# A token-mixing projection that applies the norm's token factor to its results instead of its input, on one core

## The chip, the cores and the metric

The kernel runs on one core of a Trainium2 chip, in float32. The metric is the device time of one execution in microseconds (us), as the median of several runs.

## What is computed

The reference is one layer of a decoder trunk on 256 tokens of width 2048. It has three sub-layers: a token mixer, a cross-attention into 256 memory tokens, and a gated MLP. The change touches the mixer, whose input is normed and then projected:

```
def rms_norm(x, g):
    y = xf * lax.rsqrt(jnp.mean(xf * xf, axis=-1, keepdims=True) + EPS)
    return (y * g)
z = rms_norm(x, ln_mix_pre) @ w_in      # columns: short conv, RWKV-7, retention, sparse attention, gates
```

The four groups of columns feed four mixers: a gated short convolution ("sc"), RWKV-7 ("rw", "zw", "za"; its recurrence is worked in chunks of 64 tokens, and its output is head-normed, scaled, given a bonus term and multiplied by a gate), retention ("rq", "rk", "rv", "rg") and sparse attention ("kv", "q"). The last group holds the merge gates ("g0" and the gates made in the merge loop), which go through a sigmoid. The norm has two factors: one for each input channel (g) and one for each token, rstd = rsqrt(mean(x²) + eps). The token factor is the same for all channels, so it may stand on the result: (x·rstd·g) @ w = rstd · ((x·g) @ w).

## The kernel before

Activations lie transposed, with channels on the 128 partitions and 256 tokens in the free dimension; x is 16 such tiles (`xT`). Every float32 product is made of three fast ones: a weight half is rounded by ScalarE ("high", L1179), VectorE subtracts that from the raw weight ("low", L1897), and TensorE multiplies high x (high and low of the input, side by side in 512 columns; L437) and low x high (256 columns; L442). ScalarE copies the second 256 columns of the bank out of PSUM (`mix_cross`, L1213), and VectorE adds them to the first (`evict`, L1952, which counts `chunk_out`).

A chunk is one tile of 128 output columns: 1 MB of weights, in two halves of 512 KB that cover 8 input tiles each. SyncE issues the loads (L336) in the order of the chunks, each half once the low part of the half two chunks earlier is done. The list `MIX` sets the order of the 78 chunks: 0 to 11 rw, 12 zw, 13 za, 14 and 15 rw, 16 to 27 sc, 28 to 33 kv, 34 to 37 cmp (a small product on the keys), 38 to 41 q, 42 to 45 rq, 46 to 49 rk, 50 to 57 rv (tokens on partitions, L407 and L410), 58 to 65 rg, 66 to 77 g0. On each engine `go(n, h)` stands in a list written out by hand and means "all halves before half h of chunk n"; what stands between two such calls is the mixers' own work. TensorE runs a chunk's matmuls once the chunk two before it is evicted.

The start (functions `gained`, `added`, `normed`, `x_low`, L1972 to 2025) goes: four quarters of x arrive; ScalarE squares them (L1170); VectorE multiplies two quarters by g (L1975) and sums the squares (L1981, L2004, L2006); TensorE sums over the partitions (L773); ScalarE takes the root (`std`, L1162), VectorE the reciprocal (L1884); VectorE norms x (L1988, L1888), ScalarE rounds it (L1191), VectorE makes the low part (L1996). Then TensorE can begin chunks 0 and 1, which are interleaved by quarters of the input (L450, L456).

The RWKV work is spread over chunks 4 to 45: the token shift (POOL `difference` L1762, DVE `token_shift` L1907), the key norm (ACT L1239, POOL L1767, PE `rw_kk`), the low-rank maps (`rw_lora`), the bonus sum (`rw_bonus`, L530, in the middle of chunk 20, which waits for L2094), the recurrence, and the ending of its output on VectorE: L2335 (times the reciprocal deviations), L2337 (four instructions, lnx_g and lnx_b), L2340 (plus bonus), L2343 (times the gate). Right after it VectorE works the attention units u = 0 to 7 in chunks 46 to 58: TensorE makes scores (L706, L707), VectorE the mask and the maximum (`unit_max`, L2252 to 2256), ScalarE the exponentials (L1360, L1363), VectorE scales them (`unit_scale`, to L2268), TensorE transposes them (`unit_T`, L714 to 716). The short convolution (L1784 to 1790) and one product of the retention's rotation (L1809, on 2048 columns) run on POOL. After the mixing chunks come the merge of three tiles and the merge loop over 13 tiles (four gate chunks and two branch chunks each, L894 and L903), the output projection, the cross-attention and the MLP, which the change leaves alone.

## Time and profile before

| | us |
|---|---|
| median of 3 runs | 2244.86 (2240.94 to 2255.99) |
| the profiled execution | 2244.42 |
| its span, first to last instruction | 2242.6 |
| TensorE busy with matmuls | 2190.3 |
| VectorE busy | 1503.8 |
| ScalarE busy | 1114.9 |
| GpSimd busy | 217.7 |

The profile is of one execution. Its busy time counts an engine's instructions, waits left out; its span is shorter than the execution's time by 1.8 us, which lie around it. A busy TensorE is not TensorE at its peak.

### The profile page before, as it was taken

Reading aid. Unit: us, or ns where it says so; the run is one execution under the profiler, and the core shown is the slowest. Engines: PE = TensorE matmul, PEld = TensorE weight load, DVE = VectorE, ACT = ScalarE, POOL = GpSimd, SP = SyncE. Lnnn points to the kernel's source line nnn. Section 1 sums busy time; section 2 is a strip of 40 time slices with the busy share of each in tenths; the row PEclk is TensorE's granted clock in tenths of the full one; section 3 lists DMA queues with packets and bytes.
Section 4 is the critical chain, followed back from the end, with each engine's and each line's share of the span. In section 5 each row is a group of like instructions: output and inputs, shape, how many; then the busy total and the mean of one; then the engine's idle time right before and its main releaser. Section 6 shows DMA issues by size and latency. Waiting matters only on the chain.

```text
span 2242.6 us, 36096 instructions
## 1 busy us (share of the span) xinstructions
PE 2190.3 (98%) x13410; PEld 1895.9 (85%) x13410; DVE 1503.8 (67%) x1796; ACT 1114.9 (50%) x1541; POOL 217.7 (10%) x211
## 2 busy tenths in 40 slices
PE   6999999999999999999999999989999999999998
PEld 5888887788888888888888888878888888888886
DVE  7875557656676666676875544567777777776444
ACT  5452244445555555555444443556555555554442
POOL 0141000000000000005210000411111111110000
PEclk9999999999999999999999999999999999999999
DMA  6533333343565555566555543535555555556554
GB/s 241 183 135 114 116 134 134 140 149 124 173 204 191 188 192 188 191 217 234 186 191 180 178 164 120 197 114 195 189 188 183 195 189 189 181 185 217 194 194 147
DMA packets 110519, 393.69 MB, mean 176 GB/s; under 512 B 12272, under 2 KB 12528, under 8 KB 110032
## 3 DMA queue, kind: packets, MB, share of 16 engines
q1 hardware_dynamic: 110128, 391.10, 50.8%
q8 instruction: 71, 1.16, 0.2%
q10 hardware_dynamic: 288, 1.17, 0.2%
q14 instruction: 32, 0.26, 0.0%
HBM read 390.12 MB, written 2.10 MB: 175 GB/s over the span
## 4 chain that ended last, share of the span: by engine, by line
PE 91%; DVE 6%; ACT 2%; issue 1%; DMA 0%; DVEq 0%; SPq 0%; ACTq 0%
PE bank L894 32%; PE bank L903 17%; PE bank L437 9%; PE bank L442 5%; PE sm L894 3%; PE bank L1131 3%; PE bank L1129 3%; PE bank L1130 3%; PE sm L490 2%; PE sm L903 2%; DVE part L1897 2%; PE bank L1019 1%; PE bank L1021 1%; PE bank L1020 1%; DVE part L2659 1%
## 5 line engine op out<-in xcount | busy, mean ns | idle before, releaser
L1897 DVE TENSOR_TENSOR part<-part,part 128x1024 fp32r<-128x1024 f32 (+1 forms) x748 | 946.4, 1270 | 458.4 <-ACT part L1179 443.9
L1179 ACT ACTIVATE part<-part 128x1024 fp32r<-128x1024 f32 (+1 forms) x748 | 785.3, 1051 | 480.9 <-PE bank L903 164.5
L894 PE MATMUL bank<-part,part 128*128 128x512 f32 x3168 | 763.9, 392 | 1.0 <-DVE part L2410 1.0
L894 PEld LDWEIGHTS bank<-part,part 128*128 128x128 f32 x3168 | 580.4, 188 | 113.5 <-issue 1.8
L903 PEld LDWEIGHTS bank<-part,part 128*128 128x128 f32 x3168 | 405.1, 191 | 16.0
L903 PE MATMUL bank<-part,part 128*128 128x256 f32 x3168 | 409.7, 282 | 0.0
L437 PE MATMUL bank<-part,part 128*128 128x512 f32 (+1 forms) x1088 | 263.4, 390 | 2.0 <-DVE part L1952 1.9
L437 PEld LDWEIGHTS bank<-part,part 128*128 128x128 f32 x1088 | 195.3, 189 | 42.7 <-DVE part L1952 4.3
L1491 ACT ACTIVATE part<-bank 128x256 f32<-128x256 f32 x204 | 77.9, 382 | 259.7 <-PE bank L894 239.3
L2410 DVE TENSOR_TENSOR part<-bank,part 128x256 f32<-128x256 f32 x204 | 86.3, 423 | 111.4 <-ACT part L1491 111.1
L442 PEld LDWEIGHTS bank<-part,part 128*128 128x128 f32 x1088 | 140.7, 191 | 9.0 <-issue 3.1
L442 PE MATMUL bank<-part,part 128*128 128x256 f32 (+1 forms) x1088 | 147.4, 284 | 0.8 <-DVE part L1897 0.8
L1129 PE MATMUL bank<-part,part 128*128 128x512 f32 x352 | 137.1, 390 | 0.9 <-DVE part L1897 0.9
L1131 PE MATMUL bank<-part,part 128*128 128x512 f32 x352 | 137.0, 389 | 0.0
L1130 PE MATMUL bank<-part,part 128*128 128x512 f32 x352 | 136.9, 389 | 0.0
L1213 ACT ACTIVATE part<-bank 128x256 f32<-128x256 f32 (+1 forms) x78 | 29.1, 373 | 141.8 <-PE bank L437 131.7
L894 PE MATMUL sm<-part,part 128*128 128x512 f32 x320 | 79.2, 393 | 0.9 <-DVE part L1952 0.9
L1129 PEld LDWEIGHTS bank<-part,part 128*128 128x128 f32 x352 | 66.1, 188 | 15.0 <-issue 1.3
L1827 POOL TENSOR_TENSOR part<-part 128x256 f32<-128x256 f32 x31 | 24.7, 798 | 550.2 <-DVE part L2410 550.2
L1130 PEld LDWEIGHTS bank<-part,part 128*128 128x128 f32 x352 | 66.1, 188 | 13.8
L1131 PEld LDWEIGHTS bank<-part,part 128*128 128x128 f32 x352 | 66.1, 188 | 13.6
L1851 POOL TENSOR_TENSOR part<-part 128x256 f32<-128x256 f32 x44 | 35.3, 803 | 411.9 <-DVE part L2613 411.9
(359 smaller groups left out, 1871.9 us busy)
## 6 DMA issues: line engine op xcount, KB each, us to landing
part<-in_w_up SPq DMA_DIRECT2D x176, 512.0 KB, 3.9
part<-in_w_g SPq DMA_DIRECT2D x128, 512.0 KB, 3.9
part<-in_w_dn SPq DMA_DIRECT2D x88, 512.0 KB, 4.5
part<-in_w_out SPq DMA_DIRECT2D x32, 512.0 KB, 4.5
part<-in_w_mk SPq DMA_DIRECT2D x32, 512.0 KB, 4.5
part<-in_w_mv SPq DMA_DIRECT2D x32, 512.0 KB, 4.5
part<-in_w_q SPq DMA_DIRECT2D x32, 512.0 KB, 3.9
part<-in_w_o SPq DMA_DIRECT2D x32, 512.0 KB, 4.5
```

What stands on the lines that cost most here:

```text
L437: mm = pe.matmul(dst, w[:, 0, k, :], x, start=h == 0 and k == 0, stop=h == 1 and k == 7, skip_group_check=True)
L442: mm = pe.matmul(dst, w[:, 1, k, :], x, start=False, stop=False, skip_group_check=True)
L490: return pe.matmul(sm[rows, b, c:c + w], lhsT, rhs, start=start, stop=stop)
L894: mm = pe.matmul(dst, w[:, 0, k, :], x[:, k0 + k, :], start=start and k == 0, stop=stop and k == n - 1, skip_group_check=True)
L903: mm = pe.matmul(dst[:, T:2 * T], w[:, 1, k, :], x[:, k0 + k, 0:T], start=False, stop=stop and k == n - 1, skip_group_check=True)
L1129: pe.matmul(bank[:, s, :], x, w[:, 0, j, :], start=k0 + j == 0, stop=False, skip_group_check=True)
L1130: pe.matmul(bank[:, s, :], x, w[:, 1, j, :], start=False, stop=False, skip_group_check=True)
L1131: mm = pe.matmul(bank[:, s, :], g[:, k + j, T + s * P:T + (s + 1) * P], w[:, 0, j, :], start=False, stop=k0 + j == FT - 1, skip_group_chec ...
L1179: act.activation(wsplit[(2 * m + h) % 4][:, 0, 0:n, :], raw[:, m % 2, h, 0:n, :], cp) .then_inc(sem("hi_done"), 1)
L1491: act.activation(cross[:, b, :], bank[:, b, T:2 * T], cp).then_inc(sem("cross_out"), 1)
L1897: tt(w[:, 1, 0:n, :], raw[:, m % 2, h, 0:n, :], w[:, 0, 0:n, :].bitcast(f32), SUB).then_inc(sem("lo_done"), 1)
L2410: tt(dst, bank[:, b:b + 1, 0:T], cross[:, b:b + 1, :], ADD).then_inc(sem("prod_out"), 1)
```

## The change

1. The inputs of chunks 0 and 1 are made from x as it arrives. ScalarE rounds x·g tile by tile (16 instructions with g as their scale), VectorE makes the low part in 16 instructions. The loads of x and of the first two chunks' weights are interleaved, and so are the first halves of chunks 0 and 1.
2. The squares, their sums, the root and the reciprocal are made later: squares on ScalarE after the 16 roundings, sums on VectorE after `go(2)`, the sum over partitions on TensorE at `go(4)`, root and reciprocal at `go(4)`.
3. Groups of evicted results are multiplied by rstd on VectorE (`scaled`, `scaled_shift`; 19 groups in the mixing chunks and one of 4 tiles for each of the 13 tiles of the merge loop). Consumers wait for the semaphore `scaled` in place of `chunk_out`. For rv, which has tokens on partitions, rstd is turned by two small matmuls into a column (`rcol`), which the copy and the eviction apply.
4. The ending of the RWKV output (L2335 to 2343) moves from before the attention units to behind `unit_scale` of units 0, 1 and 2.

```diff
 @block.sync
+            load_x(0)
+            load_half(0, 0, A["w_rw"][MIX[0][1]])
+            load_half(1, 0, A["w_rw"][MIX[1][1]])
+            load_x(1)
+            load_x(2)
+            load_half(0, 1, A["w_rw"][MIX[0][1]])
+            load_half(1, 1, A["w_rw"][MIX[1][1]])
+            load_x(3)
 @block.tensor
-            pe.wait_ge(sem("x_sum"), 1)
-            pe.matmul(sm[:, 5, 0:T], ones, sq0[:, 0, :], start=True, stop=True).then_inc(sem("norm_mm"), 1)
...
-            go(7)
+            go(4)
+            pe.wait_ge(sem("x_sum"), 1)
+            pe.matmul(sm[:, 5, 0:T], ones, sq0[:, 0, :], start=True, stop=True).then_inc(sem("norm_mm"), 1)
+            go(7, 1)
             pe.wait_ge(sem("consts_loaded"), 16)
             rw_kk()
+            go(10)
+            pe.wait_ge(sem("rstd_ready"), 1)
+            for t in range(2):
+                mm = pe.matmul(sm[:, 5, t * P:t * P + 64], rstd[:, t * P:(t + 1) * P], cc("ident")[:, 0:64],
+                               start=True, stop=True)
+            mm.then_inc(sem("rstd_turned"), 1)
 @block.scalar
+            def x_high(q):
+                act.wait_ge(sem(f"x_loaded{q}"), 16)
+                for k in range(4 * q, 4 * q + 4):
+                    act.activation(H[:, k, 0:T], xT[:, k, :], cp, scale=vv("ln_mix_pre", k)).then_inc(sem("hsplit_high"), 1)
+            x_high(0)
             high(0, 0, one)
             high(1, 0, one)
             x_high(1)
+            x_high(2)
+            high(0, 1, one)
             high(1, 1, one)
             x_high(3)
+            for q in range(4):
+                act.activation(sq0[:, 4 * q:4 * q + 4, :], xT[:, 4 * q:4 * q + 4, :], ACT.Square) \
+                   .then_inc(sem("x_sq"), 1)
...
+            go(4)
+            std(1)
+            go(6)
             rw_kk()
...
 @block.gpsimd
-                pool.wait_ge(sem("chunk_out"), AT[("sc", 3 * i + 2)] + 1)
+                pool.wait_ge(sem("scaled"), SCALED["sc", i])
...
-            pool.wait_ge(sem("chunk_out"), AT[("rk", 3)] + 1)
+            pool.wait_ge(sem("scaled"), SCALED["rk", 0])
             pool.wait_ge(sem("rw_yc"), 3)
             pool.tensor_tensor(rt1, rqk, bc(trig[:, 0, 0, :], 8), MUL).then_inc(sem("ret_cos"), 1)
 @block.vector
+            def x_low(q):
+                for k in range(4 * q, 4 * q + 4):
+                    dve.wait_ge(sem("hsplit_high"), k + 1)
+                    mm = stt(H[:, k, T:2 * T], xT[:, k, :], vv("ln_mix_pre", k), H[:, k, 0:T].bitcast(f32), MUL, SUB)
+                mm.then_inc(sem("hsplit_low"), 1)
+            def scaled(key, last, x, n):
+                dve.wait_ge(sem("chunk_out"), AT[last] + 1)
+                tt(x, x, bc(rstd[0:x.shape[0], :], n), MUL).then_inc(sem("scaled"), 1)
...
+            x_low(0)
+            low(0, 0, one)
+            low(1, 0, one)
+            x_low(1)
+            x_low(2)
+            low(0, 1, one)
+            low(1, 1, one)
+            x_low(3)
+            go(2)
+            for q in range(1, 4):
+                added(q)
...
+            go(4)
+            dve.wait_ge(sem("norm_std"), 1)
+            mark(dve.reciprocal(rstd[:, :], rstd[:, :]), "rstd_ready", 1)
+            scaled_shift(0)
+            go(5)
             token_shift(0)
...
             go(44, 1)
-            link(tt(Yc, Yc, Nm, MUL))
-            for i in range(4):
-                mm = ts(s4(Yc)[:, i, :], s4(Yc)[:, i, :], vv("rw_lnx_g", i), vv("rw_lnx_b", i), MUL, ADD)
-            link(mm)
-            go(45)
-            link(tt(Yc, Yc, bonus, ADD))
             go(45, 1)
             cmp_p()
-            mark(tt(obr_rw, s4(Yc), s4(gl), MUL), "rw_yc", 3)
...
                 unit_scale(u)
+                rw_output(u)
+                if u == 4:
+                    scaled("rq", ("rq", 3), rqk[:, 0:4, :], 4)
+                elif u == 6:
+                    scaled("rk", ("rk", 3), rqk[:, 4:8, :], 4)
```

The other groups are scaled on VectorE at these places: shift 1 (rw 0 to 3) behind `go(8)`; shift 2 before `go(13)`; shift 3 (zw and za) behind `go(14)`; shift 4 behind `go(16)`; sc 0 behind `go(20)`, sc 1 behind `go(22, 1)`, sc 2 behind `go(25)`, sc 3 behind `go(28)`; kv 0 (2 tiles) behind `go(30)` and kv 1 (4 tiles) behind `go(34)`; q behind `go(42)`; rg 0 behind `go(62)` and rg 1 behind `go(66)`; g0 behind `go(70)`, `go(74)` and after the last chunk. In the merge loop the multiplication of the four gate tiles stands behind the fourth gate chunk's eviction, and ScalarE's sigmoid waits for it.

## Rows read from the trace of the kernel before

**Rows 1.** The page's first part: busy us (share of span) xinstructions

```profile
PE 2190.3 (98%) x13410; PEld 1895.9 (85%) x13410; DVE 1503.8 (67%) x1796; ACT 1114.9 (50%) x1541; POOL 217.7 (10%) x211
```

**Rows 2.** Busy time in three stretches: start, attention units, all after mixing

```profile
0.00:21.00 21.00, 1.44 (x3) 0.72 (x4) 13.97 (x13) 10.78 (x12) 1.58 (x10) 1.00 0.63 238
...
371.00:470.00 99.00, 91.84 (x517) 73.74 (x517) 63.01 (x106) 50.38 (x121) 4.57 (x1) 0.98 0.40 141
...
625.00:2242.00 1617.00, 1597.61 (x8674) 1385.77 (x8672) 1084.18 (x1277) 834.56 (x1121) 159.64 (x157) 1.00 0.54 185
```

**Rows 3.** What TensorE waited for: total us, times, longest us

```profile
PE sm L773 <- DVE part L2006: 13.6, 1, 13.6
PE sm L714 <- DVE part L2268: 7.1, 5, 3.8
```

**Rows 4.** Timeline of the start: start us, us, engine, line, tiles, count [idle before]

```profile
4.85 1.06 ACT L1170 ACTIVATE part<-part 128x1024 f32<-128x1024 f32 x1 [2.11 <-DMA part<-in_xT]
...
7.49 1.22 DVE L1981 TENSOR_TENSOR part<-part 128x1024 f32<-128x1024 f32 x1 [0.25 <-ACT part L1170]
...
8.95 1.06 ACT L1170 ACTIVATE part<-part 128x1024 f32<-128x1024 f32 x1 [0.22 <-DMA part<-in_xT]
...
12.40 0.69 DVE L2004 TENSOR_TENSOR part<-part 128x512 f32<-128x512 f32 x1
13.12 0.42 DVE L2006 TENSOR_TENSOR part<-part 128x256 f32<-128x256 f32 x1
...
15.37 1.75 DVE L1884 RECIPROCAL rstd<-rstd 128x256 f32<-128x256 f32 x1 [0.56 <-ACT rstd L1162]
...
20.78 6.65 PE L450 MATMUL bank<-part,part 128*128 128x512 f32 x16 [5.96 <-DVE part L1996]
...
28.21 3.82 PE L450 MATMUL bank<-part,part 128*128 128x512 f32 x16
...
31.87 3.04 PE L456 MATMUL bank<-part,part 128*128 128x256 f32 x24
...
44.06 3.82 PE L437 MATMUL bank<-part,part 128*128 128x512 f32 x16
...
47.72 2.08 PE L442 MATMUL bank<-part,part 128*128 128x256 f32 x16
...
49.92 1.66 DVE L1907 SCALAR_TENSOR_TENSOR part<-part,vec 128x256 f32<-128x256 f32 x4
...
52.90 1.69 ACT L1239 ACTIVATE part<-part,vec 128x256 f32<-128x256 f32 x4
```

**Rows 5.** Timeline around the bonus sum in chunk 20

```profile
145.75 1.65 POOL L1784 TENSOR_TENSOR part<-part 128x256 f32<-128x256 f32 x1 [0.88 <-DVE part L1952]
...
148.40 2.10 DVE L2094 SCALAR_TENSOR_TENSOR part<-part,vec 128x256 f32<-128x256 f32 x4
...
150.65 1.96 PE L530 MATMUL sm<-part,cst 128*128 128x512 f32 x4 [1.87 <-DVE part L2094]
```

**Rows 6.** Timeline around attention unit 0

```profile
359.24 1.39 DVE L2337 TENSOR_SCALAR part<-part,vec 128x256 f32<-128x256 f32 x4
...
374.97 0.48 PE L714 MATMUL sm<-cst,part 128*128 128x128 f32 x1 [3.82 <-DVE part L2268]
...
376.17 3.05 PE L437 MATMUL bank<-part,part 128*128 128x512 f32 x8
```

**Rows 7.** Busy time in one us of unit 0 (PEclk is the third number from the end)

```profile
375.00:376.00 1.00, 1.00 (x5) 1.00 (x6) 1.00 (x1) 0.55 (x1) 0.00 (x0) 0.50 0.54 205
```

**Rows 8.** Timeline around attention unit 3

```profile
402.34 4.57 POOL L1809 TENSOR_TENSOR part<-part,part 128x2048 f32<-128x2048 f32 x1 [90.76 <-DVE part L1952]
...
403.78 4.22 DVE L1897 TENSOR_TENSOR part<-part,part 128x1024 fp32r<-128x1024 f32 x1 [1.52 <-ACT part L1179]
```

**Rows 9.** TensorE's timeline at chunk 70, and VectorE's at unit 7

```profile
553.92 2.11 PE L437 MATMUL bank<-part,part 128*128 128x512 f32 x8 [0.74 <-DVE part L1952]
...
456.45 0.43 DVE L2252 TENSOR_TENSOR sm<-sm,cst 128x256 f32<-128x256 f32 x1 [1.74 <-PE sm L707]
```

**Rows 10.** Timeline of a tile of the merge loop, after its fourth gate chunk

```profile
645.79 1.23 DVE L1897 TENSOR_TENSOR part<-part,part 128x1024 fp32r<-128x1024 f32 x1 [0.52 <-ACT part L1179]
```

More of the change, by code:

```diff
@@ L128, with split_at @@
           (14, 16, P, ("rw", 13)))
+SCALED = [("shift", 0), ("shift", 1), ("shift", 2), ("shift", 3), ("shift", 4), ("sc", 0), ("sc", 1), ("sc", 2), ("sc", 3),
+          ("kv", 0), ("kv", 1), ("q", 0), ("rq", 0), ("rk", 0), ("rg", 0), ("rg", 1), ("g0", 0), ("g0", 1), ("g0", 2)]
+SCALED = {key: n + 1 for n, key in enumerate(SCALED)}
+def split_at(m, h):
+    return 2 * m + h + 1 if m >= 2 else 2 * h + m + 1
 M_BR = NMIX
@@ L322, in _, with load_x @@
         def _(sp):
-            for q in range(4):
+            def load_x(q):
                 sp.dma_start(xT[:, 4 * q:4 * q + 4, :], A["xT"][:, 4 * q:4 * q + 4, :]).then_inc(sem(f"x_loaded{q}"), 16)
@@ L353, in _ @@
                 j = {"zw": 0, "za": 1, "g0": i // 4}.get(what, i)
-                load(n, A[src][j], one)
+                if n >= 2:
+                    load(n, A[src][j], one)
                 if n == 6:
@@ L624, in nsa_dup @@
             def nsa_dup():
-                pe.wait_ge(outd, AT[("kv", 1)] + 1)
+                pe.wait_ge(sem("scaled"), SCALED["kv", 0])
                 for kv in range(2):
@@ L741, in ret_rot @@
                 pe.wait_ge(sem("nsa_o"), 4)
+                pe.wait_ge(sem("scaled"), SCALED["rk", 0])
                 for j in range(4):
@@ L1212, in mix_cross @@
                     s, d = bank[:, n % 2, T:2 * T], cross[:, n % 2, :]
-                act.activation(d, s, cp).then_inc(sem("mix_cross"), 1)
+                if what == "rv":
+                    act.activation(d, s, cp, scale=rcol[:, i % 2:i % 2 + 1]).then_inc(sem("mix_cross"), 1)
+                else:
+                    act.activation(d, s, cp).then_inc(sem("mix_cross"), 1)
             at_half = [0]
@@ L1247, in rw_lora_in @@
             def rw_lora_in():
-                act.wait_ge(outd, AT[("za", 0)] + 1)
+                act.wait_ge(sem("scaled"), SCALED["shift", 3])
                 act.activation(gsig[96:120, :], zp[96:120, 13, 1:257], ACT.Sigmoid).then_inc(sem("rw_lora_in"), 1)
@@ L1760, in difference @@
                 a, b, rows, last = SHIFTS[m]
-                pool.wait_ge(sem("chunk_out"), AT[last] + 1)
+                pool.wait_ge(sem("scaled"), SCALED["shift", m])
                 pool.tensor_tensor(Z[0:rows, a:b, :], zp[0:rows, a:b, 0:256], zp[0:rows, a:b, 1:257], SUB) \
@@ L1951, in evict @@
                     d = g0[:, i // 4, i % 4, :]
-                tt(d[0:rows], s[0:rows], c[0:rows], ADD).then_inc(sem("chunk_out"), 1)
+                if what == "rv":
+                    stt(d, s, rcol[:, i % 2:i % 2 + 1], c, MUL, ADD).then_inc(sem("chunk_out"), 1)
+                else:
+                    tt(d[0:rows], s[0:rows], c[0:rows], ADD).then_inc(sem("chunk_out"), 1)
             at_half = [0]
@@ L2097, in _ @@
             mark(dve.tensor_copy(WC.unsqueeze(2), g16(dW)[:, :, 63:64]), "rw_ready", 2)
+            scaled("sc", ("sc", 2), scb[:, 0], 3)
             go(21)
@@ L2121, in _ @@
             tt(g16(Xm), bc(cc("eye64"), 16), g16(P1), SUB)
+            scaled("sc", ("sc", 5), scb[:, 1], 3)
             go(23)
@@ L2134, in _ @@
             ts(g16(Bt), wide(0), -1.0, None, MUL).then_inc(sem("rw_s4_out"), 1)
+            scaled("sc", ("sc", 8), scb[:, 0], 3)
             def level(n):
@@ L2277, in _ @@
             level2(2)
+            scaled("sc", ("sc", 11), scb[:, 1], 3)
             go(29)
@@ L2281, in _ @@
             level2(3)
+            go(30)
+            scaled("kv", ("kv", 1), kvr[:, 0:2, :], 2)
             go(30, 1)
@@ L2295, in _ @@
             go(34)
+            scaled("kv", ("kv", 5), kvr[:, 2:6, :], 4)
             u_out(0)
@@ L2322, in _ @@
             go(42)
+            scaled("q", ("q", 3), qn, 4)
             dve.wait_ge(sem("rw_std"), 1)
@@ L2334, in _, with rw_output @@
             go(44, 1)
[L2335 to L2340 removed]
             go(45, 1)
             cmp_p()
[L2343 to L2344 removed]
+            def rw_output(step):
+                if step == 0:
+                    link(tt(Yc, Yc, Nm, MUL))
+                    for i in range(4):
+                        mm = ts(s4(Yc)[:, i, :], s4(Yc)[:, i, :], vv("rw_lnx_g", i), vv("rw_lnx_b", i), MUL, ADD)
+                    link(mm)
+                elif step == 1:
+                    link(tt(Yc, Yc, bonus, ADD))
+                elif step == 2:
+                    mark(tt(obr_rw, s4(Yc), s4(gl), MUL), "rw_yc", 3)
+                    dve.sem_inc(sem("branches"), 1)
             for u in range(8):
@@ L2358, in _ @@
             go(62)
+            scaled("rg", ("rg", 3), rg[:, 0:4, :], 4)
             dve.wait_ge(sem("ret_mm"), 2)
@@ L2370, in _ @@
             go(66)
+            scaled("rg", ("rg", 7), rg[:, 4:8, :], 4)
             dve.wait_ge(sem("ret_mm"), 5)
@@ L2393, in _ @@
             obr_low(obr_nsa, 4, 16, 3)
+            go(70)
+            scaled("g0", ("g0", 3), g0[:, 0], 4)
             go(70, 1)
@@ L2397, in _ @@
             dve.sem_inc(sem("branches"), 2)
+            go(74)
+            scaled("g0", ("g0", 7), g0[:, 1], 4)
             go(NMIX)
+            scaled("g0", ("g0", 11), g0[:, 2], 4)
             def ma_low(h):
```

100 lines of the change are left out of this document (37 added, 63 removed).

## The prediction

> **What bounds the kernel now.** I read the page first: TensorE is busy for 2190.3 of 2242.6 us [rows 1], so only what takes TensorE's work or its 52 us of idleness away can count. Then busy time by stage, to see where those 52 us lie: the first 21 us hold 19.6 of them (1.44 us of matmul), the attention units 7.2, everything after the mixing chunks 19.4 in 1617 us [rows 2]. Then the waits of TensorE: 13.6 us before the sum of squares (L773) and 7.1 us before the transposes of the attention units (L714) [rows 3]. Last the timelines of those places. At the start TensorE does nothing for chunks until 20.78 us, because squares, sums, root, reciprocal and norming stand in a chain between the arrival of x at 4.85 to 8.95 us and the first low part [rows 4]. From chunk 2 on a chunk costs TensorE 5.57 us (16 matmuls of 512 columns in 3.65 and 16 of 256 in 1.92, the spacing in the rows of 3.82 and 2.08) against about 2.9 us of VectorE (two low halves at 1.23, an eviction at 0.42); VectorE therefore has room almost everywhere, except where the mixers' own work is packed: chunk 20, the way into unit 0, and chunks 66 to 71 [rows 5, 6, 9].
>
> **The start (parts 1 and 2).** A quarter of x (512 KB) lands every (8.95 − 4.85) / 3 = 1.37 us [rows 4]; a weight half is as big. In the new order they land at about: x0 4.9, first half of chunk 0 6.3, of chunk 1 7.7, x1 9.0, x2 10.4, second halves 11.8 and 13.1, x3 14.4. ScalarE: a quarter is 4 instructions with a scale, 1.69 us, and a weight half 1.05 us [rows 4], a half being as wide as L1170. Starting at 5.1: x0 6.8, halves 7.9 and 8.95, x1 10.65, x2 12.35, halves 13.4 and 14.5, x3 16.15. VectorE needs 1.66 us for a quarter's low part (L1907's form) and 1.23 for a half: 7.3, 9.1, 10.3, 12.0, 13.7, 14.9, 16.1, 17.8. So TensorE starts at 7.9 in place of 20.78 and its last quarter is ready at 17.8. Its first 16 matmuls took 0.416 us each and the next 16 0.23: the lower of its two levels until it had worked 6.65 us [rows 4]. I let it run slowly for as long here: first quarter to 11.2, second 12.0 to 14.9, first low products 15.9, third quarter 17.7, fourth 17.8 to 19.65, the last three groups of low products 2.9: done at 22.5.
>
> Chunk 2 waits for its predecessor on ScalarE, which now squares x first (4 × 1.06): 16.15 + 4.2 = 20.4, high half 21.4, low half 22.6, eviction of chunk 0 at 23.0. TensorE starts chunk 2 at 23.0, chunk 3 at 28.6. VectorE sums the squares there: 3 × 1.22 + 0.69 + 0.42 = 4.8 us [rows 4]; the 0.69 is a sum of 512 columns between these two until 30.7; the last low half of chunk 3 is then 0.5 us late. With the sum over partitions (0.5) chunk 4 starts at 23.0 + 11.1 + 1.0 = 35.2. In the profile of before the chunk that starts in the middle of the row at 44.06 is chunk 4: 44.06 + 1.83 = 45.9. **The start gives −10.7 us.** Bounds: −13 if the squares don't hold up chunk 2 and nothing is late, −5 if TensorE stays on its lower level through both chunks (its 64 matmuls then need 20 us from 7.9, done at 28.4 and not 22.5).
>
> The root and the reciprocal (1.75) and the first scaled group (1.22) end on VectorE near 39.2, while TensorE has chunk 4's lows since 34.7 and needs chunk 5's second low at 43.6: hidden. Token shift, key norm and their POOL parts follow some 3 us later relative to the chunks than before, and the change gives the products behind them half a chunk more (`go(7, 1)`). The turned rstd adds two small matmuls, +0.2.
>
> **The groups scaled (part 3).** VectorE pays 1.22 for four tiles, about 0.95 for three, 0.69 for two: in the mixing chunks some 21 us in all, in the merge loop 13 × 1.22 = 16 us. Where it has over 2 us of slack per chunk this reaches nobody. In the merge loop the multiplication pushes the low half at 645.79 by 1.22 − 0.52 = 0.7 us [rows 10]; TensorE is four matmul groups away from it. I take 0 there; bounds 0 to +6. On the way to the bonus sum, TensorE waited 1.87 us for L2094, four instructions that took 2.10 in place of 1.66 while POOL ran the short convolution [rows 5, 4]; the low half before it was stretched as well, by 0.4. The short convolution now waits for its scaling behind `go(20)`, so it starts after L2094: −0.85. The kv group stands ahead of a small copy that TensorE's recurrence waits for, +0.1. At chunks 66 to 71 VectorE is the limit already (TensorE waits 0.74 for an eviction at chunk 70 [rows 9], and twice 0.4 around it): rg's second group adds 1.2 ahead of the retention's reciprocals, and g0's first group adds 1.22 between two chunks, of which I count 0.7: +1.9. Bounds 0 and +2.4.
>
> **The RWKV ending (part 4).** Ahead of unit 0 VectorE works without a pause, and four steps leave it: 1.22 + 1.39 + 1.22 + 1.22 = 5.1 us [rows 4, 6]. The scaled q adds 1.22, in a place with 1.4 us of idleness behind it. Unit 0's scaling ends at 374.9 and TensorE has waited 3.82 us. I replay it without the four steps: ScalarE's table load and exponential then hold VectorE to 362 for the next low half, and the maximum is done at 368.0 in place of 371.7, the exponentials at 369.8, the scaling at 371.3: the wait shrinks to 0.2, −3.6. After the wait the granted clock was 0.50 for some three us [rows 7], and eight matmuls took 3.05 in place of 2.0, the six transposes before them 1.2 in place of 0.6 [rows 6]: −1.7 more, if a wait of 0.2 costs no clock. Sum −5.3; bounds 0 (the wait moves to ScalarE or to unit 1) and −5.5. The moved steps land behind unit_scale of units 0, 1, 2 with 2.65, 1.22 and 1.22 us, where VectorE idled 2.9 us before the next scores: hidden, unit 0's with 0.3 to spare.
>
> In unit 3 the POOL product L1809 (4.57) ran into a low half, which took 4.22 in place of 1.23, and TensorE then waited 0.94 us [rows 8, 3]. It waits for the scaled rk now and so runs at unit 7: −0.9 at unit 3. At unit 7 VectorE had 1.5 + 1.74 us idle [rows 9]; 1.22 goes to rk and 3.0 to POOL's stretch: +1.0. Bounds 0 and +2.5.
>
> The upper bound has a rule behind it. The Trainium skill, page "SBUF — State Buffer", section "Who interferes with whom", says that a VectorE instruction with two SBUF inputs and a GpSimd instruction that reads SBUF block each other for a whole instruction, whichever came first. Rows 8 fit: the low half ended 1.1 us after POOL did. By that rule the low half, which starts together with POOL here and not 1.4 us behind it, would lose 4.5 in place of 3.0, and the sum would be 2231.4.
>
> **Sum.** −10.7 + 0.2 − 0.85 + 0.1 + 1.9 − 5.3 − 0.9 + 1.0 = −14.5 us. From the profiled execution's 2244.42 (span 2242.6 and 1.8 around it) that is 2229.9, I say 2230. The median of before, 2244.86, is 0.4 above the profiled execution, so nothing need be shifted. The remaining 1.6 ms are bound by TensorE and untouched; what is won at the front stays won.
>
> **Rivals.**
> 1. The wait at unit 0 only moves. For it: ScalarE there has a table load, an exponential, two PSUM copies and four exponentials in a row, and units 1, 3, 5 and 6 waited 0.8 us each although nothing was piled up on VectorE. Against it: VectorE's queue is unbroken for 20 us ahead of unit 0. Price: 4 of the 5.3 us come back, 2234.
> 2. The start is slow: TensorE stays low, or the load order makes chunk 2 wait. For it: there are pauses between the quarters. Against it: none is over 1 us by my replay. Price: +5.9 (above), 2236.
> 3. More is won: scaling on results also empties ScalarE and VectorE at the start so that chunk 2 follows at once, and POOL's move relieves chunks 20 and 49 fully. −2.3 at the start, −1 at chunk 20, −1 at 550: 2225.5.
> 4. Slower than before: the scalings become TensorE's. VectorE gets 37 us of new work; where its list is late, an eviction or a low half is late and TensorE waits as at chunk 70 [rows 9]. It decides once more than 37 × 0.4 = 15 us come through; if all of the merge loop's 16 and half of the 21 did and the waits lowered the clock as in rows 7 once (1.7), the time is 2230 + 16 + 10.5 − 1.9 + 1.7 = 2256. Against it: the merge loop's idle slots of 0.9 and 1.3 us each chunk.
>
> **Chances.** The forecast 0.60, rival 1 0.13, rival 2 0.10, rival 3 0.12, rival 4 0.05. The range 2220 to 2240 takes in rivals 1 to 3 and some 4 us of terms that I have not found on either side. One per cent is 22.4 us, about what a measurement can tell from no change: faster by over 1% (below 2222.4) needs rival 3 and more, 0.11; within 1% 0.85; slower by over 1% 0.04.
>
> **What would show it.** First matmul of a chunk near 8 us, chunk 2's first near 23, chunk 4's near 35 (each right or wrong by itself). TensorE's wait for L773 gone; its longest wait at L714 under 1 us, with no stretch at a granted clock of 0.50 behind it. POOL's 2048-column product near 440 us with a stretched low half beside it, and a wait at unit 7. The wait ahead of the bonus sum near 1 us. About 2 us of waits more at chunks 66 to 72, none in the merge loop. The forecast is wrong if chunk 4 starts after 39, or if TensorE waits over 5 us in the merge loop.

## The result, and the profile after

The changed kernel takes 2228.90 us in the median (2227.78 to 2229.68), the kernel before 2244.68 beside it: a ratio of 0.9923 (95% interval 0.9900 to 0.9945). The forecast was 2230, in 2220 to 2240. The profiled execution took 2229.68 us with a span of 2227.9, so its trace is 14.7 us shorter than the one of before.

The first part of the page, in the columns of [rows 1]:

```profile
PE 2189.3 (98%) x13414; PEld 1893.6 (85%) x13414; DVE 1532.7 (69%) x1830; ACT 1119.2 (50%) x1553; POOL 223.1 (10%) x211
```

TensorE has 4 matmuls more and the same work. VectorE works 29 us longer and TensorE does not notice. The three stretches of [rows 2], in the changed kernel's times:

```profile
0.00:21.00 21.00, 12.51 (x51) 9.69 (x52) 11.15 (x20) 16.67 (x27) 1.59 (x10) 1.00 0.88 318
371.00:470.00 99.00, 94.90 (x536) 75.95 (x536) 66.53 (x100) 47.93 (x104) 5.48 (x1) 1.00 0.41 140
625.00:2227.00 1602.00, 1582.88 (x8594) 1372.59 (x8592) 1088.62 (x1277) 829.33 (x1113) 159.72 (x157) 1.00 0.56 185
```

The first 21 us hold 12.5 us of matmul in place of 1.4. After the mixing chunks TensorE is idle for 19.1 us in place of 19.4. What TensorE waits for now, answering to [rows 3]:

```profile
PE bank L475 <- ACT part L1209: 8.3, 1, 8.3
...
PE sm L740 <- DVE part L2313: 4.0, 4, 1.5
```

The 13.6 us before the sum of squares are gone and 8.3 us before the first matmul stand in their place. The waits at the attention's transposes (now L740) fell from 7.1 to 4.0 us, the longest from 3.8 to 1.5. The start, answering to [rows 4]:

```profile
5.55 1.71 ACT L1219 ACTIVATE part<-part,vec 128x256 fp32r<-128x256 f32 x4 [2.81 <-DMA vec<-in_vec]
...
8.35 6.68 PE L475 MATMUL bank<-part,part 128*128 128x512 f32 x16 [8.35 <-ACT part L1209]
...
16.09 1.67 DVE L2022 SCALAR_TENSOR_TENSOR part<-part,vec,part 128x256 fp32r<-128x256 f32 x4
16.28 3.89 ACT L1230 ACTIVATE part<-part 128x1024 f32<-128x1024 f32 x4
...
22.76 2.14 PE L462 MATMUL bank<-part,part 128*128 128x512 f32 x8
...
30.29 2.45 PE L467 MATMUL bank<-part,part 128*128 128x256 f32 x16
...
34.66 2.19 PE L462 MATMUL bank<-part,part 128*128 128x512 f32 x8
```

The first row waits for the vectors, not for x. Chunk 2 starts at 22.76 (forecast 23.0) and chunk 4 at 34.66 (35.2) against 45.9 before. From chunk 4's second matmul on the difference is 11.1 us and not 11.2, since the last of the sum's matmuls overlaps the first one. (The expectations below give 34.86 for chunk 4's first matmul; the row's 34.66 is the value to compare with.)

Matched matmul by matmul from the end backwards, the two traces give the size of each term (us):

| place | forecast | trace |
|---|---|---|
| start, up to chunk 4 | -10.7 | -11.07 |
| turned rstd | +0.2 | +0.48 |
| chunk 14, groups scaled there | 0 | +0.33 |
| bonus sum, chunk 20 | -0.85 | -0.88 |
| kv ahead of a copy | +0.1 | +0.03 |
| attention unit 0 | -5.3 | -5.30 |
| unit 3 | -0.9 | -0.84 |
| unit 7 | +1.0 | +1.42 |
| chunks 66 to 71 | +1.9 | +1.78 |
| merge loop | 0 | 0 |
| the clock's dip near 1475 us | not told | -0.85 |
| small shifts | not told | +0.17 |
| sum | -14.5 | -14.73 |

The clock's dips (stretches at a granted clock of 0.50) are as long in both traces: 3.4 us near 290 us and 10.2 us near 1475 us (286 and 1488 in the kernel before). The second one lies over other matmuls and waits than before, and costs 0.85 us less.

### The profile page after: what moved, and what is told of

Same layout as the page of the kernel before. It is cut to its first block, busy times and chain, and to the rows that moved or that the text cites. A ratio compares the mean times of both kernels' runs of the same rounds, so it can differ in the third digit from the quotient of the medians.

```text
span 2227.9 us, 36155 instructions
## 1 busy us (share of the span) xinstructions
PE 2189.3 (98%) x13414; PEld 1893.6 (85%) x13414; DVE 1532.7 (69%) x1830; ACT 1119.2 (50%) x1553; POOL 223.1 (10%) x211
## 4 chain that ended last, share of the span: by engine, by line
PE 91%; DVE 5%; ACT 2%; issue 1%; DMA 0%; DVEq 0%; SPq 0%; ACTq 0%
PE bank L927 32%; PE bank L936 17%; PE bank L462 9%; PE bank L467 5%; PE sm L927 3%; PE bank L1162 3%; PE bank L1164 3%; PE bank L1163 3%; PE sm L515 2%; PE sm L936 2%; DVE part L1935 2%; PE bank L1053 1%; PE bank L1054 1%; PE bank L1052 1%; DVE part L2729 1%
## 5 line engine op out<-in xcount | busy, mean ns | idle before, releaser
L1164 PEld LDWEIGHTS bank<-part,part 128*128 128x128 f32 x352 | 66.1, 188 | 13.7
```

Of the source, the lines that this page charges most:

```text
L1164: mm = pe.matmul(bank[:, s, :], g[:, k + j, T + s * P:T + (s + 1) * P], w[:, 0, j, :], start=False, stop=k0 + j == FT - 1, skip_group_chec ...
```

## The experiments

Fourteen traces are compared: of before, of the changed kernel (twice) and of eleven others. Ratios are against the kernel before, timed beside each; its median was 2243.5 to 2244.5.

**1. Part 4 undone (undo_ending).** All four steps of the recurrence's ending stand ahead of the attention units again, the rest of the change stays.

```diff
             go(44, 1)
+            link(tt(Yc, Yc, Nm, MUL))
+            for i in range(4):
+                mm = ts(s4(Yc)[:, i, :], s4(Yc)[:, i, :], vv("rw_lnx_g", i), vv("rw_lnx_b", i), MUL, ADD)
...
-                rw_output(u)
```

> The changed kernel with part 4 undone: the four steps that end the RWKV output stand before the attention units again. My theory (VectorE's queue ahead of unit 0 sets TensorE's wait, and the wait costs the clock as well): 5.2 us more than the changed kernel's 2228.9, so 2234.1, with a wait of at least 3.6 us at unit 0 and a granted clock of 0.50 behind it. Rival 1 (the wait only moves to ScalarE or to a later unit): 2230 or less. Both expect the start and everything up to chunk 42 unchanged.

Measured: 2235.09 us (2233.62 to 2235.85), ratio 0.9954 (0.9936 to 0.9972). Unit 0 in the timeline of this kernel:

```profile
362.59 0.33 PE L740 MATMUL sm<-cst,part 128*128 128x128 f32 x1 [3.80 <-DVE part L2313]
...
363.22 3.66 PE L462 MATMUL bank<-part,part 128*128 128x512 f32 x8
```

the us from 363.5 (granted clock third from the end):

```profile
363.50:364.50 1.00, 1.00 (x4) 0.81 (x3) 0.62 (x2) 0.96 (x3) 0.00 (x0) 0.50 0.15 41
```

and the same place in the changed kernel, with the moved step behind the scaling:

```profile
359.33 0.69 DVE L2313 TENSOR_TENSOR part<-part,small 128x512 f32<-128x512 f32 x1
360.05 1.23 DVE L2391 TENSOR_TENSOR part<-part 128x1024 f32<-128x1024 f32 x1
...
360.07 0.33 PE L740 MATMUL sm<-cst,part 128*128 128x128 f32 x1
...
360.70 2.09 PE L462 MATMUL bank<-part,part 128*128 128x512 f32 x8
```

The wait of [rows 6] is back with its fall of the clock, and 5.4 us with them: 3.8 of wait, 1.6 of matmuls at the lower level. (The whole trace is only 4.2 us longer, because the dip near 290 us is missing in it, which is worth 1.5.) The first rival (the wait only moves) is refuted: nowhere behind unit 0 does the changed kernel give them back.

**2. Part 4 alone, on the kernel before (ending_alone).** The converse of the first.

```diff
-            link(tt(Yc, Yc, Nm, MUL))
...
                 unit_scale(u)
+                rw_output(u)
```

> The kernel of before with part 4 alone. My theory: the ending's gain does not depend on the rest of the change; 2244.7 - 5.3 = 2239.4, first wait for the transposes under 0.5 us, no stretch at a granted clock of 0.50 behind it, the wait of 0.94 us at unit 3 still there because POOL's product stays at chunk 49. Rival 1: 2244, the same wait a unit later.

Measured: 2241.62 us (2239.68 to 2243.28), ratio 0.9991 (0.9981 to 1.0000). Its trace is only 2.9 us shorter than the one of before. Unit 0 gave its 5.3 us, and unit 3 took 2.9 of them back, so part 4 was worth 2.4 us. (The rest is 0.5 from the start; a dip near 299 us of 6.8 us in place of 3.4 cost 1.5, and a shorter one near 1490 us gave 1.4.) Unit 3:

```profile
396.43 1.23 DVE L2348 TENSOR_TENSOR part<-part 128x1024 f32<-128x1024 f32 x1
...
399.44 4.56 POOL L1809 TENSOR_TENSOR part<-part,part 128x2048 f32<-128x2048 f32 x1 [86.78 <-DVE part L1952]
...
399.52 5.56 DVE L1897 TENSOR_TENSOR part<-part,part 128x1024 fp32r<-128x1024 f32 x1 [0.16 <-ACT part L1179]
...
410.29 0.33 PE L714 MATMUL sm<-cst,part 128*128 128x128 f32 x1 [2.26 <-DVE part L2268]
```

GpSimd's product waits for chunk 49's eviction (L1952), which the last moved step (the first row) has put off on VectorE by its 1.23 us. ScalarE's rounding was not put off, so the product starts 0.08 us ahead of a low half where it had a lead of 1.44 [rows 8], and the low half takes 5.56 us in place of 4.22. The wait at unit 3 grew from 0.94 to 2.26 us and the granted clock was 0.50 behind it:

```profile
412.00:413.00 1.00, 1.00 (x5) 0.90 (x4) 0.00 (x0) 0.07 (x1) 0.00 (x0) 0.50 0.33 111
```

Neither theory had this, so it was tried in 3.

**3. Part 4 alone, and GpSimd's product held back (ending_pool_later).**

```diff
             pool.wait_ge(sem("chunk_out"), AT[("rk", 3)] + 1)
+            pool.wait_ge(sem("nsa_pv_mm"), 8)
             pool.wait_ge(sem("rw_yc"), 3)
```

> The kernel before with part 4 alone (the ending of the recurrence's output between the attention units, as in the run ending_alone) and with GpSimd's product of 128x2048 held until the attention's eighth product, so that it runs behind the last unit. In ending_alone that product started at 399.44 and a low half beside it took 5.56 us, ahead of unit 3's softmax, whose matmul waited 2.26 us (0.94 in the kernel before). Theory (part 4 gains its 5.3 us at unit 0, and ending_alone lost 2.9 of them only because the product met a low half ahead of unit 3): no wait at unit 3, trace 5.3 + 0.9 = 6.2 us shorter than before less 0.2 for the moved instructions, time 2244.3 - 6.0, about 2238.3. Rival (the moved steps themselves, queued ahead of unit 3 on VectorE, are what is late there): the wait of 2.3 us and the dip of the clock stay, time about 2241.5 as in ending_alone.

Measured: 2238.01 us (2234.45 to 2248.24), ratio 0.9974 (0.9960 to 0.9988), the trace 6.4 us shorter than the one of before (a longer dip of the clock near 299 us cost 1.5 of it, a shorter one near 1490 us gave 1.3, the start 0.5). Unit 3:

```profile
399.53 1.22 DVE L1898 TENSOR_TENSOR part<-part,part 128x1024 fp32r<-128x1024 f32 x1 [0.15 <-ACT part L1179]
...
408.14 0.33 PE L714 MATMUL sm<-cst,part 128*128 128x128 f32 x1
```

The low half takes 1.22 us again, TensorE does not wait, and unit 3 gives 0.85 us on top of unit 0's 5.3. So the moved steps are hidden, and part 4 alone is worth 5.3 us only if the product stands elsewhere. In the change part 3 does this, with no word of it: the product now waits for the scaled rk. The sum treated the two parts as independent, and came out right because both were made: that was luck.

**4. No group multiplied (no_scaling).** All multiplications of groups by the token's factor are left out, their semaphores stay (rv keeps its column). The first of three such places:

```diff
                 dve.wait_ge(sem("chunk_out"), AT[last] + 1)
-                tt(x, x, bc(rstd[0:x.shape[0], :], n), MUL).then_inc(sem("scaled"), 1)
+                dve.sem_inc(sem("scaled"), 1)
...
```

> The changed kernel with every multiplication of a group by the token factor left out (some 37 us of VectorE's work; the semaphores are still counted, rv still gets its column factor). My theory (the scalings are hidden except at chunks 66 to 71, 1.6 us, at chunk 14, 0.3 us, and partly at unit 7): 2.5 us less than 2228.9, so 2226.4, and nothing gained in the merge loop. Rival 4 (the scalings become TensorE's time wherever VectorE's list is late): 10 us or more less, 2219 or below, most of it in the merge loop.

Measured: 2227.45 us (2226.06 to 2228.03), ratio 0.9922 (0.9903 to 0.9941); the trace 2.1 us shorter than the changed kernel's, 2.4 until the dip near 1475 us, of which 0.3 came at chunk 14, 0.6 at unit 7 and 1.5 at chunks 65 to 71. The multiplications are some 37 us of VectorE's instructions (its busy time falls from 1532.7 to 1500.8) and cost TensorE under 3 us: the fourth rival, 15 us and more, is refuted. Not all waits at 66 to 71 are theirs. First the changed kernel, then this one:

```profile
535.74 1.18 PE L467 MATMUL bank<-part,part 128*128 128x256 f32 x8 [1.09 <-DVE part L1935]
539.51 2.11 PE L462 MATMUL bank<-part,part 128*128 128x512 f32 x8 [0.75 <-DVE part L1993]
```

```profile
533.88 1.18 PE L467 MATMUL bank<-part,part 128*128 128x256 f32 x8 [0.60 <-DVE part L1935]
537.65 2.12 PE L462 MATMUL bank<-part,part 128*128 128x512 f32 x8 [0.75 <-DVE part L1993]
```

The 0.75 of the second row is not the multiplications' doing, and neither is a wait of 0.49 at 543.06 (541.21 in this kernel).

**5. GpSimd's product behind the last unit (pool_later).** The wait of 3, put into the changed kernel.

> The changed kernel with POOL's 2048-column product (the cosine part of the retention's rotation) held back until the last unit's value products, out of the attention units. My theory (the product blocks a VectorE low half and so delays unit 7's maximum): the wait at unit 7 falls from 1.51 us to 0.3 or less, 1.2 us less than 2228.9, so 2227.7. Rival (the multiplication of rk, 1.22 us on VectorE in the same place, makes the wait): the wait stays over 1 us and the time at 2228.9.

Measured: 2228.53 us (2226.37 to 2230.50), ratio 0.9926 (0.9905 to 0.9946). The time does not tell the theories apart; the trace does. Unit 7 of the changed kernel:

```profile
434.49 1.22 DVE L1935 TENSOR_TENSOR part<-part,part 128x1024 fp32r<-128x1024 f32 x1
434.65 5.48 POOL L1847 TENSOR_TENSOR part<-part,part 128x2048 f32<-128x2048 f32 x1 [134.16 <-DVE part L2028]
...
436.40 4.80 DVE L1935 TENSOR_TENSOR part<-part,part 128x1024 fp32r<-128x1024 f32 x1 [0.30 <-ACT part L1209]
...
446.43 0.33 PE L740 MATMUL sm<-cst,part 128*128 128x128 f32 x1 [1.51 <-DVE part L2313]
```

and with the product held back:

```profile
438.14 1.23 DVE L1936 TENSOR_TENSOR part<-part,part 128x1024 fp32r<-128x1024 f32 x1 [0.30 <-ACT part L1209]
...
446.75 0.33 PE L740 MATMUL sm<-cst,part 128*128 128x128 f32 x1
...
451.99 5.62 POOL L1848 TENSOR_TENSOR part<-part,part 128x2048 f32<-128x2048 f32 x1 [149.77 <-PE sm L762]
```

The wait at unit 7 is gone, though rk is still multiplied there, and the trace gains 1.4 us. Before that it had lost 1.6 near 290 us, in code that is the same in both: the dip of the clock there lasted 6.8 us and not 3.4.

**6. Other places for two groups (regrouped).** The product as in 5, and on VectorE (ScalarE's sigmoid moves along):

```diff
+            go(65)
+            dve.wait_ge(sem("chunk_out"), AT[("rg", 6)] + 1)
+            tt(rg[:, 4:7, :], rg[:, 4:7, :], bc(rstd[:, :], 3), MUL)
             go(66)
-            scaled("rg", ("rg", 7), rg[:, 4:8, :], 4)
+            scaled("rg", ("rg", 7), rg[:, 7:8, :], 1)
...
-            go(70)
-            scaled("g0", ("g0", 3), g0[:, 0], 4)
...
+            go(72)
+            scaled("g0", ("g0", 3), g0[:, 0], 4)
```

> The changed kernel with GpSimd's product behind the last unit (as in pool_later), three of the last four rg chunks multiplied one chunk earlier, where VectorE idles for 3.3 us, and the first group of g0, with its sigmoid, moved from chunk 70 to chunk 72, where VectorE idles for 0.6 to 1.3 us between its instructions. No arithmetic is left out. In no_scaling leaving the multiplications out took 0.8 us off at chunk 65 to 66 and 0.7 more up to chunk 71, and pool_later took 1.3 off at unit 7. Theory (at chunks 66 to 71 VectorE is behind, and only what stands there costs): 1.3 at unit 7 and 1.2 to 1.7 up to chunk 72, trace 2.5 to 3.0 shorter than the changed kernel's apart from what the clock's dips do, time about 2226.3. Rival (the waits at 66 to 71 come of the ending of the retention and of the roundings, the multiplications only share in them): only the 1.3 at unit 7, time about 2227.7.

Measured: 2228.09 us (2225.95 to 2229.57), ratio 0.9927 (0.9906 to 0.9947). The time lies nearer to the rival's 2227.7 than to the theory's 2226.3, and its spread takes in both; the places are read from the trace. It gains 1.4 us at unit 7 and 1.3 between chunks 65 and 71, as the theory had it, and ends 0.1 us shorter than the changed kernel's, because a dip of 6.8 us near 275 had cost 3.2, of which the missing dip near 290 gave 1.5 back. The busy time from 276 us on:

```profile
276.00:278.00 2.00, 2.00 (x20) 1.78 (x20) 0.73 (x3) 1.06 (x1) 0.00 (x0) 0.50 0.25 86
```

In the changed kernel the granted clock of these 2 us is 1.00.

**7. TensorE busy before x comes (warm_start).**

```diff
+            pe.wait_ge(sem("eps_set"), 2)
+            for _ in range(15):
+                pe.matmul(sm[:, 5, 0:P], ones, ones, start=True, stop=True)
```

> The changed kernel with fifteen matmuls of the ones tile by itself (128x128, into a bank that nothing reads) on TensorE's queue ahead of its first chunk, in the time in which it waits for the token's first quarter. In the changed kernel the first twelve matmuls of 512 columns stand 0.43 us apart and the later ones 0.23, and the last eight of them start at 17.82, behind the last quarter's VectorE part. Theory (the start ends with the last quarter's arrival and its two roundings, TensorE's slow first matmuls are hidden): chunk 4's first matmul stays within 0.4 us of 34.86, and the time stays at 2229, within 1. Rival (the slow clock of the first matmuls sets the start): 12 matmuls at 0.20 less each, chunk 4's first matmul 2.4 us earlier, time about 2226.5.

Measured: 2229.57 us (2228.72 to 2231.62), ratio 0.9937 (0.9915 to 0.9959). The start in the timeline:

```profile
8.18 2.41 PE L475 MATMUL bank<-part,part 128*128 128x512 f32 x8 [0.64 <-ACT part L1212]
12.23 2.09 PE L475 MATMUL bank<-part,part 128*128 128x512 f32 x8 [1.64 <-DVE part L2025]
...
17.84 2.12 PE L475 MATMUL bank<-part,part 128*128 128x512 f32 x8 [0.73 <-DVE part L2025]
...
22.76 2.11 PE L462 MATMUL bank<-part,part 128*128 128x512 f32 x8
```

The first matmuls are twice as fast, and chunk 2 starts at 22.76 as before: what was saved is waited for, 1.64 us for the second quarter and 0.73 for the last. The slow clock of the start is hidden behind the arrival of x. The rival is refuted. (The trace ends 1.0 us shorter, by the missing dip near 290 us, 1.5, and one near 1475 us that costs 0.5 more.)

**8. The same, with another order at the start (start_both).** The last quarter of x ahead of the second weight halves in the load, on ScalarE and on VectorE; the squares one by one between the roundings. The edit of the load:

```diff
             load_x(2)
-            load_half(0, 1, A["w_rw"][MIX[0][1]])
-            load_half(1, 1, A["w_rw"][MIX[1][1]])
             load_x(3)
+            load_half(0, 1, A["w_rw"][MIX[0][1]])
+            load_half(1, 1, A["w_rw"][MIX[1][1]])
```

> The changed kernel with the same fifteen matmuls and another order at the start: the token's last quarter is loaded, rounded and multiplied ahead of the second halves of the first two chunks; chunk 0 is finished before chunk 1's second half; the squares of the token stand behind the first roundings on ScalarE, one after each, and the constants' load behind the third. Theory (both together remove what the start waited for, and TensorE itself becomes the bound): after the second quarter at 14.1 TensorE needs 8 low matmuls (0.95), 16 high (3.7) and 24 low (2.9) in a row, so chunk 2 starts at about 21.6 and not 22.76, and chunk 4's first matmul comes 1.2 us earlier than 34.86; time about 2227.7. Rival (VectorE and ScalarE set the pace of chunks 2 and 3 anyway, through the sums of squares and the roundings): chunk 4's first matmul within 0.4 us of 34.86, time 2229.

Measured: 2230.42 us (2228.62 to 2231.40), ratio 0.9938 (0.9917 to 0.9958). The rival was right, in its mechanism too. Chunk 2 starts at 22.20, 0.56 us early, and chunk 3 pays it back: its second low half stands behind three additions of squares on VectorE. Chunk 4 starts at 35.19.

```profile
25.75 3.73 DVE L2032 TENSOR_TENSOR part<-part 128x1024 f32<-128x1024 f32 x3
...
30.70 2.36 DVE L1951 TENSOR_TENSOR part<-part,part 128x1024 fp32r<-128x1024 f32 x2
...
32.08 1.19 PE L467 MATMUL bank<-part,part 128*128 128x256 f32 x8 [1.35 <-DVE part L1951]
```

**9. The additions spread, the constants' load later (start_three),** and quarter and half in turn. The edit of the additions:

```diff
-            go(2)
-            for q in range(1, 4):
-                added(q)
+            go(1)
+            added(1)
+            go(1, 1)
+            added(2)
+            go(2)
+            added(3)
```

> The changed kernel with the start of start_both and three things more: token quarter 1 comes ahead of chunk 1's first half and quarter 2 and 3 between the second halves, each on TensorE as soon as it is there; the additions of the squares stand one by one between the low halves of chunks 2 and 3 on VectorE and not three in a row (3.73 us there in start_both, ahead of a low half for which TensorE waited 1.35 us); the constants' 863 KB are loaded behind chunk 4's roundings. Theory (start_both lost its 1.2 us to VectorE's three additions and to the constants' transfer): chunk 2 starts at about 21.4 and not at 22.76, no wait of over 0.2 us follows up to chunk 4, chunk 4's first matmul is 1.4 to 1.8 us earlier than 34.86, time about 2227.4. Rival (the weights' transfers bound the start): waits for ScalarE behind a DMA take the place of those for VectorE, chunk 4's first matmul within 0.5 us of 34.86, time 2229.

Measured: 2230.03 us (2228.80 to 2231.59), ratio 0.9937 (0.9924 to 0.9951). The wait at chunk 3 is gone, and chunk 4 starts at 34.30, 0.36 us early and not 1.4 to 1.8. The rival's number fits and its reason does not: ahead of chunk 4 ScalarE waits 0.50 and 0.37 us for quarters of x and never for a weight half, and TensorE waits for no transfer. Chunk 2 starts at 22.89, though TensorE works in one piece from 14.22 us on; the granted clock was 0.50 from 11.5 us on for 3.4 us, behind waits of 1.90 and 1.58 us. Such a dip costs 1.5 us near 290 us; as much would explain why chunk 2 does not start at the 21.4 of the theory.

**10. Experiments 6 and 9 in one kernel (all_in_one), and the changed kernel again beside it (after_again).** Its edits are those shown above.

> The start of start_three and the groups and the product placed as in regrouped, all arithmetic kept. If both act as they do alone: 1.6 us at the start, 1.3 at unit 7 and 1.1 at chunks 65 to 72, so a trace about 4.0 us shorter than the changed kernel's where the clock's dips are the same, time about 2225. Rival (gains at the start are taken back by the chunks' transfers before chunk 20): 2.4 us, time about 2226.5.

> The changed kernel once more, unchanged, beside the two below on the same chip. Every theory expects 2229 within 1 us. What differs from its first trace is what one trace cannot tell: the dip of the clock near 290 us has lasted 0, 3.4 or 6.8 us in traces of programs whose work there is the same, so the trace may differ by about 1.7 us either way.

Measured on one chip: the changed kernel 2229.66 us (2228.97 to 2230.35), ratio 0.9935 (0.9921 to 0.9949); all in one 2225.67 us (2224.52 to 2228.48), ratio 0.9919 (0.9905 to 0.9932). All its times lie below all of the changed kernel's beside it (the intervals of the ratios overlap), and the median is near the 2225 of the theory. Its trace is not: it is 1.2 us shorter than the changed kernel's and not 4.0. Unit 7 and chunks 65 to 71 give 2.7 where 2.4 were expected, but chunk 4 starts at 35.68, 1.0 us late, with the granted clock at 0.50 from 10.4 us on for 6.8 us. The profiled execution is the slowest of the five (2228.48).

**11. TensorE's gaps at the start filled (all_filled).** All in one, with eighteen fillers ahead and five behind the first four matmuls:

```diff
+                if q == 0:
+                    fill(5)
```

> all_in_one with eighteen instead of fifteen matmuls of the ones tile ahead of the first chunk and five more behind its first four matmuls, where TensorE waited 1.59 us for VectorE; nothing else differs. In the trace of all_in_one the granted clock was 0.50 from 10.4 us on, for 6.8 us, and chunk 2 started at 24.27 and not at the 21.4 that the matmuls add up to at 0.23 each. Theory (the new start order was right, and lost its gain to the fall of the clock behind TensorE's waits of 0.93 and 1.59 us): no dip before 280 us, chunk 2 at 21.5 to 21.8, chunk 4's first matmul 2.4 to 2.8 us earlier than all_in_one's 35.68, the trace 2.5 us shorter than all_in_one's, time about 2223.5. Rival (what holds the start is the transfers and VectorE's order, the clock only fills their gaps): chunk 4's first matmul at 35 or later, time 2225.5.

Measured: 2225.37 us (2224.66 to 2228.06), ratio 0.9919 (0.9905 to 0.9932), span 2222.9. From 12 to 16 us in all_in_one, then here:

```profile
12.00:16.00 4.00, 4.00 (x14) 3.46 (x14) 3.84 (x8) 3.88 (x9) 0.00 (x0) 0.50 0.99 389
```

```profile
12.00:16.00 4.00, 4.00 (x25) 3.49 (x24) 3.66 (x8) 3.83 (x9) 0.00 (x0) 1.00 0.98 388
```

TensorE is busy for all 4 us in both, and starts 14 matmuls in one and 25 in the other. Chunk 4 starts at 33.40, 2.3 us ahead of all_in_one and 1.3 ahead of the changed kernel:

```profile
22.00 2.00 PE L462 MATMUL bank<-part,part 128*128 128x512 f32 x8
...
33.40 2.19 PE L462 MATMUL bank<-part,part 128*128 128x512 f32 x8
```

In this pair of traces that is the theory, a little short (2.4 to 2.8 expected). The trace is 3.8 us shorter than all_in_one's: 2.3 at the start and 1.5 from the missing dip near 290 us. The median is only 0.3 us below all_in_one's, inside the spread of either, and misses the theory's 2223.5. That all_in_one's other executions had a shorter dip at the start or none would explain it: their mean granted clock was 0.995 to 0.997, and 0.994 in the profiled one. Where along the kernel the difference lies was not seen, so it is not shown that the fillers save time in most executions. The median is 3.5 us below the changed kernel's first one and 4.3 below its second, neither timed beside it.

## Why the prediction was right

The time came out 1.1 us below the forecast (0.3 in the second set, 2229.66), and the sum's terms stand where they were put: the start and unit 0 carry 16.4 us of the gain, chunk 20 and unit 3 another 1.7, and four places (turned rstd, chunk 14, unit 7, chunks 66 to 71) give 4.0 back, where 3.1 were forecast. That the sum meets the trace within 0.2 us is in part luck: the 0.85 us of the dip near 1475 us, which no term foresaw, make up for that.

**The start.** Right in its working: the last quarter is ready at 17.8 as forecast, so the slow clock costs nothing (experiment 7), and the sums of squares hold up the last low half of chunk 3 (0.4 us late, forecast 0.5). That the squares hold up chunk 2 is true by 0.1 us and not by the 0.5 of the forecast: chunk 0 is evicted at 22.71, and TensorE's own work on chunks 0 and 1 is done at about 22.6 (24 matmuls from 19.76 on, 0.12 us apart). What it had 0.45 us too early, the first rounding (5.55 and not 5.1, since it waits for the vectors' transfer), is without effect for the same reason: the last quarter landed at 14.66, forecast 14.4.

**Chunk 14.** "Where it has over 2 us of slack per chunk this reaches nobody" is the step that failed, by 0.3 us. First the kernel before, then the changed one, at the same work:

```profile
104.00 0.42 DVE L1952 TENSOR_TENSOR part<-bank,part 120x256 f32<-120x256 f32 x1
...
104.50 1.95 POOL L1762 TENSOR_TENSOR part<-part 96x512 f32<-96x512 f32 x1 [9.19 <-DVE part L1952]
...
105.59 1.95 DVE L1897 TENSOR_TENSOR part<-part,part 128x1024 fp32r<-128x1024 f32 x1
...
110.70 2.08 PE L442 MATMUL bank<-part,part 128*128 128x256 f32 x16
```

```profile
96.87 0.42 DVE L1993 TENSOR_TENSOR part<-bank,part 120x256 f32<-120x256 f32 x1
...
98.16 1.96 POOL L1800 TENSOR_TENSOR part<-part 96x512 f32<-96x512 f32 x1 [8.39 <-DVE part L2035]
...
99.25 1.95 DVE L1935 TENSOR_TENSOR part<-part,part 128x1024 fp32r<-128x1024 f32 x1
...
100.11 2.41 PE L467 MATMUL bank<-part,part 128*128 128x256 f32 x16
```

In both kernels GpSimd's difference runs ahead of a low half, which takes 1.95 us in place of 1.23: that is nothing new. New is how late VectorE is. Before, this low half ended at 107.54, and the ninth matmul of TensorE's row, the first that needs it (the profile names no releaser here, the times say so), started at 111.65, 4.1 us later. Now it ends at 101.20 and the ninth matmul starts right behind, at 101.34, 0.3 us late. Without the multiplications (experiment 4) the low half ended at 98.86, 2.4 us ahead of its matmul (101.28), and the 0.3 us were gone. So of 4.1 us of lead the multiplications of this and the earlier chunks took some 2.5 and the later start of the mixers' work the rest. The forecast had both (it let that work follow "some 3 us later relative to the chunks") and did not add them up: VectorE's slack is a lead that is used up over several chunks, not an allowance in each.

**Bonus sum.** Right for the stated reason: the four instructions took 1.66 us in place of 2.10, the low half before them 1.22 in place of 1.65, the wait fell from 1.87 to 1.00, and the short convolution starts behind them, at 142.13. This is read from the rows; no run changes this wait alone.

```profile
137.72 1.66 DVE L2136 SCALAR_TENSOR_TENSOR part<-part,vec 128x256 f32<-128x256 f32 x4
...
139.53 1.95 PE L556 MATMUL sm<-part,cst 128*128 128x512 f32 x4 [1.00 <-DVE part L2136]
```

**Unit 0.** Right, place and price (3.8 of wait and 1.5 of clock, forecast 3.6 and 1.7), shown from both sides (experiments 1 and 2). The replay left 0.2 us of wait; there is none.

**Unit 3.** 0.84 for 0.9. Here the forecast did not ask what the moved steps do to the product's neighbour: with the product in its old place they cost 2.9 us (experiment 2), and only part 3 spared them.

**Unit 7.** The mechanism was right and its size off: 1.4 us in place of 1.0. The product started 0.16 us behind one low half and ahead of the next. The first kept its 1.22 us, the product took 5.48 in place of 4.57, and the second low half 4.80: VectorE lost 3.6 us there, where 3.0 were forecast. The Trainium skill ("SBUF — State Buffer", "Who interferes with whom") has the two blocking each other for a whole instruction in order of issue, and every case here agrees: the first low half ended at 435.71 and the product 4.42 us later at 440.13 (4.57 by itself [rows 8]); the low halves that had to wait ended 1.07 (here), 1.08 (chunk 14) and 1.09 us [rows 8] behind GpSimd. In experiment 2 it was 1.08. The 2.5 us that the forecast put beside the rule were too high only because it had one low half meet the product from its start; a first one slipped in ahead.

**Chunks 66 to 71.** 1.8 us for 1.9; experiment 6 shows that 1.3 of it is a matter of place.

**Turned rstd, kv.** 0.48 and 0.03 for 0.2 and 0.1.

**The rivals.** The first and fourth are refuted by experiments 1 and 4, the second by chunk 2's start and experiment 7. The third (2225.5) was not what happened, but a time close to it was to be had with all arithmetic kept, by order and fillers: 2225.7 in experiment 10 and 2225.4 in experiment 11.

## What to carry to other kernels

Ask of every semaphore whose producer is moved or delayed what the waiting GpSimd instruction will now run beside: here changed waits removed 0.9 us at chunk 20 and 0.8 at unit 3 and added 1.4 at unit 7, and the place of one product decided whether another edit was worth 5.3 or 2.4 us. A second engine's slack hides new work well (37 us for under 3), except where its list is already late; there the place matters more than the amount. Count that slack as a lead that earlier work uses up (chunk 14), not chunk by chunk. A faster start is worth what the last operand allows: filling TensorE's gaps did nothing alone, and with another order 2.3 us in one pair of traces and nothing clear in the median.

## What was not expected of the hardware

The granted clock of TensorE falls in places where no wait tells it. Near 275 to 305 us, in the small matmuls, the dip to 0.50 lasted 3.4 us in the kernel before and in both traces of the changed one, 6.8 us in five kernels of this study and 0 in three (14 traces, six with 3.4), though that stretch of code is the same in all of them, and TensorE was busy for 34.00 of the 34 us from 274 us on in each. From 3.4 to 0 us the trace gained 1.5 (experiments 1, 7 and 11), from 3.4 to 6.8 it lost 1.6 (experiments 5 and 9). One pair of traces therefore does not settle a difference of 3 us in the span; the place where it arises does.

At the start, waits of 0.93 and 1.59 us with little work between them went ahead of a fall (experiment 10), and so did one of 2.26 us at unit 3 (experiment 2), while four waits at the attention units of up to 1.5 us passed without. So did 0.64 and 1.64 us (experiment 7) and 0.88 and 1.65 us (experiment 8) at the start, with eight matmuls of 512 columns between them and not four.

While TensorE was on its lower level from the first instruction on (matmuls of 512 columns 0.43 us apart from 8.35 to 13.7 us in the changed kernel), the view gives the granted clock of that stretch as 1.00; only the spacing of the matmuls shows it.
